# The triangular solve of a gated delta rule: products and subtractions of half the columns

## The chip, the cores and the metric

The kernel runs on one core of a Trainium2 chip. A core has a matrix engine (TensorE, PE in the profile; its weight loads are listed apart, as PEld), a vector engine (VectorE, DVE), an activation engine (ScalarE, ACT), a general engine (GpSimd, POOL), and a sync engine (SyncE, SP) that starts the transfers. Matrix products read their two operands from the on-chip memory SBUF and write to the accumulator memory PSUM, which has 8 banks of 512 fp32 columns on 128 partitions. The metric is the device time of one execution in microseconds; lower is better.

## The reference, cut to what matters

The model is a two-layer trunk that runs over 1024 prompt tokens and 64 tokens of a continued stream. The second layer mixes tokens with a gated delta rule of 8 heads, computed in chunks of 64 tokens:

```python
m = jnp.where(strict, jnp.einsum('bhnid,bhnjd->bhnij', kb, k) * decay, 0.0)
a = m + jnp.eye(L, dtype=f32)
rhs = jnp.concatenate([v * beta[..., None], kb * jnp.exp(G)[..., None]], -1)
sol = lax.linalg.triangular_solve(a, rhs, left_side=True, lower=True, unit_diagonal=True)
w_val, k_cd = sol[..., :dv], sol[..., dv:]
...
def step(st, inp):
    qd, kcd, wv, at, kt, gt = inp
    v_new = wv - jnp.einsum('bhld,bhde->bhle', kcd, st)
    o = jnp.einsum('bhld,bhde->bhle', qd, st) + jnp.einsum('bhij,bhje->bhie', at, v_new)
    st = st * gt[..., None, None] + jnp.einsum('bhld,bhle->bhde', kt, v_new)
    return st, o
```

For each head and chunk a unit lower triangular 64 x 64 matrix `a` has to be inverted. Around this lie the projections, the attention of the first layer and two convolutional feed-forward networks.

## The kernel before

The program is a row of blocks: the first projections, attention, a layer block (`eo`), the delta block (`delta_block`, line 2804), and a second layer block (`oo`). Outside the delta block the work is long rows of matrix products.

**The delta block** takes the chunks in pairs: `Pair(0)` to `Pair(7)` hold two chunks of the prompt each (`nb` = 2, J = 8 matrices on each half of the partitions), `Pair(8)` holds the one chunk of the continued stream (`nb` = 1). Every engine has its own function `run(A, B, C)`, called by `stages` for successive pairs: A is the pair whose matrix is being inverted, B the pair before, whose state update is made, C the pair after, whose inputs are prepared. The order on each engine is the order of the code, and the engines meet at semaphores. Head h of 0 to 3 lies on partitions 0 to 63, head h + 4 on partitions 64 to 127 (`places`), so that two 64 x 64 products run side by side. A chunk is `b`, and `HALVES[b]` are its four matrices per half.

**The inverse** is built by doubling. `T` holds the inverse of the diagonal blocks, `TT` (`solved(A)`) its transpose. Block size 2 is done by masks, then levels l = 1 to 5 double it. At level l, for each chunk b:

- PE, line 3236 ("X product"): `X = ML[l-1]^T T`, 8 products of 64 x 64, to PSUM;
- ACT, line 3339: copies X to SBUF;
- PE, line 3250: the update of T, and line 3253: the update of TT, 8 products each, into the two halves of PSUM bank 6 + b. At level 5 only the second is made;
- DVE, lines 3465 and 3466: subtract them from T and from TT. One semaphore, `Y`, is raised after both groups of a chunk.

PE first issues the X products of both chunks, then the updates of both. It waits for `T` of the chunk before its X products, and for `TT` and the copy `Xs` before its updates. An fp32 product shows as two weight loads and two matmuls in the trace, so a group of 8 products is `x16`.

Between the levels other work is queued on the engines. On DVE `differences(C)` (lines 3376, 3378, 3379) stands after level 1, and `normed(B)` (line 3405) after level 5. On PE `squares_sum(B)` (line 3152) stands after level 2, and the next pair begins with line 3184. On ACT stand `squares_o`, `squares_q`, the decays, `root_o`, `squares_k` and `rms`. POOL makes line 3061 and the masks `ML` (line 2997), scales q (line 3069), and prepares C. In the last pair PE makes some products of the next block (`early`, lines 160 to 166) before and after the X product of level 5.

Of the kernel before, what the change touches and what calls it, by code (L numbers as in the profile page):

```python
# [7 lines left out]
ALU = mybir.AluOpType  # L8
# [64 lines left out]
def settle(eng, sem):  # L73


    eng.sem_inc(sem, 1)
# [2727 lines left out]
def delta_block(nc, ctx, m, d):  # L2804
# [7 lines left out]
    s = m.next  # L2812
    H, L = HEADS, CH
    GR = H // 2
    HALVES = (slice(0, GR), slice(GR, H))
    X_BANK = [None, 0] + [4] * (LEVELS - 2)
    with ExitStack() as mem:
# [17 lines left out]
        TT = (TT, sb("TT1", [P, H, L]))  # L2835
# [6 lines left out]
        def solved(p):  # L2842

            return GB[:, 1] if p.k == NPAIR else TT[p.odd]
# [9 lines left out]
        def bank2(b, n=P):  # L2854

            return m.ps[:, b:b + 2, :].rearrange("p b (h c) -> p (b h) c", c=P)[:, :, 0:n]

        def chunks(x, p):

            return x[:, 0:p.nb].rearrange("p b h g c -> p (b h g c)")  # L2860
# [5 lines left out]
        def bank1(b):  # L2866

            return m.ps[:, b, :].rearrange("p (h c) -> p h c", c=L)
# [223 lines left out]
        def _(pe):  # L3092
            def old_values(B, b):

                pe.wait_ge(s("kc"), B.th(1, 1))
                if not B.first:

                    pe.wait_ge(s("oln"), B.th(0, 1))
                pe.wait_ge(s("S"), B.th(b + 1, 2))
                if B.k == NPAIR:  # L3100
                    pe.wait_ge(s("S_in"), 16)
                r = B.blocks()[b]
                for h, half, j in places(b):
                    ins = pe.matmul(bank2(0)[half, j, :], kc[B.odd][:, h, r], state(B, b)[:, h, :], start=True, stop=True)
                ins.then_inc(s("kS"), 1)

                pe.wait_ge(s("qd"), B.th(1, 1))

                pe.wait_ge(s("onorm"), B.th(1, 1))
                for h in range(H):  # L3110
                    pe.matmul(bank2(2)[:, h, r], state(B, b)[:, h, :], kq[B.odd][:, h, r], start=h % GR == 0, stop=False)

            def solve(B, b):

                pe.wait_ge(s("r"), B.th(b + 1, 2))
                pe.wait_ge(s("TT"), B.th(B.group(LEVELS - 1, b), 2 * LEVELS))
                for h, half, j in places(b):
                    ins = pe.matmul(bank2(0)[half, j, :], solved(B)[half, j, :], vt[B.odd][half, j, :], start=True, stop=True)
                ins.then_inc(s("Tr"), 1)
# [51 lines left out]
            def turn(A, bank, x, name):  # L3171
                settle(pe, s("settled_pe"))
                for b in range(A.nb):
                    for hh in range(GR):
                        ins = pe.transpose(bank2(bank)[:, GR * b + hh, :],
                                           x[:, b, hh].rearrange("p g c -> p (g c)"), m.ident[:, :])
                ins.then_inc(s(name), 1)

            def run(A, B, C):
                if A:  # L3180
                    n = A.n
                    pe.wait_ge(s("sqk"), A.th(1, 1))
                    for b in range(A.nb):
                        ins = pe.matmul(bank2(4)[:, HALVES[b], :], m.ones[:, :], sq[:, HALVES[b], :],
                                        start=True, stop=True)
                    ins.then_inc(s("ksum"), 1)
                    pe.wait_ge(s("in2"), A.loaded())
                    if not A.first:

                        pe.wait_ge(s("TT"), A.th(0, 2 * LEVELS))  # L3190
                    turn(A, 6, kv, "vturned")
                if B:
                    old_values(B, 0)
                    solve(B, 0)
                if not A:
                    early(0, 2)
                if A:
                    pe.wait_ge(s("kn"), A.th(1, 1))
                    pe.wait_ge(s("vt"), A.th(1, 1))
                    gram_k(A)  # L3200
                if B:
                    state_step(B, 0, A)
                    output(B, 0)
                if A:
                    pe.wait_ge(s("in0"), A.th(16, 16))
                    gram_q(A)
                if B and B.n == P:
                    old_values(B, 1)
                    solve(B, 1)
                if A:  # L3210

                    pe.wait_ge(s("T0"), A.th(1, 1))
                    pe.wait_ge(s("AT"), A.th(1, 1))
                    turn(A, 6, kk, "kturned")
                if B and B.n == P:
                    state_step(B, 1, A)
                    output(B, 1)
                if A:

                    if B:  # L3220
                        pe.wait_ge(s("vn"), B.th(B.nb, 2))
                    for l in range(1, LEVELS):
                        pe.wait_ge(s("ML"), A.th(l, LEVELS - 1))
                        if l == 2:

                            if B:
                                pe.wait_ge(s("S"), B.th(3, 2))
                            else:
                                pe.wait_ge(s("kln"), A.th(1, 1))
                        if A.k == NPAIR and l == LEVELS - 1:  # L3230
                            early(0, 0, 1)
                        for b in range(A.nb):
                            pe.wait_ge(s("T"), A.th(A.group(l - 1, b), 2 * (LEVELS - 1)))
                            settle(pe, s("settled_pe"))
                            for h, half, j in places(b):
                                ins = pe.matmul(bank1(X_BANK[l] + b)[half, j, :], ML[half, l - 1, j, :], T[half, j, :],
                                                start=True, stop=True)
                            ins.then_inc(s("X"), 1)
                        if A.k == NPAIR and l == LEVELS - 1:
                            early(0, 1, 2)  # L3240
                        if l == 1:

                            pe.wait_ge(s("kscaled"), A.th(A.nb, 2))
                        for b in range(A.nb):
                            pe.wait_ge(s("TT"), A.th(A.group(l - 1, b), 2 * LEVELS))
                            pe.wait_ge(s("Xs"), A.th(A.group(l - 1, b), 2 * (LEVELS - 1)))
                            settle(pe, s("settled_pe"))
                            if l < LEVELS - 1:
                                for h, half, j in places(b):
                                    pe.matmul(bank1(6 + b)[half, j - GR * b, :], solved(A)[half, j, :], X[half, j, :],  # L3250
                                              start=True, stop=True)
                            for h, half, j in places(b):
                                ins = pe.matmul(bank1(6 + b)[half, GR + j - GR * b, :], X[half, j, :], solved(A)[half, j, :],
                                                start=True, stop=True)
                            ins.then_inc(s("Y"), 1)
                        if B and l == 2:
                            squares_sum(B)
                elif B:
                    early(1)
                    squares_sum(B)  # L3260
                    pe.wait_ge(s("oln"), B.th(1, 1))
                    early(2)
# [107 lines left out]
        def _(dve):  # L3370
# [37 lines left out]
            def run(A, B, C):  # L3408
                if A:
                    n, J, tt = A.n, A.J, solved(A)  # L3410
# [47 lines left out]
                if A:  # L3458
                    for l in range(1, LEVELS):
                        for b in range(A.nb):  # L3460
                            hs = HALVES[b]
                            y = bank1(6 + b)
                            dve.wait_ge(s("Y"), A.th(A.group(l - 1, b), 2 * (LEVELS - 1)))
                            if l < LEVELS - 1:
                                dve.tensor_tensor(T[:, hs], T[:, hs], y[:, 0:GR], ALU.subtract).then_inc(s("T"), 1)
                            dve.tensor_tensor(tt[:, hs], tt[:, hs], y[:, GR:H], ALU.subtract).then_inc(s("TT"), 1)
                        if l == 1 and C:

                            dve.wait_ge(s("kscaled"), A.th(A.nb, 2))
                            dve.wait_ge(s("AT"), A.th(1, 1))  # L3470
                            differences(C)
                        if B and l == rms_level(A):
                            normed(B)
                elif B:
                    normed(B)
# [120 lines left out]
```

## Time and profile before

| | us |
|---|---|
| time, median of 3 runs | 2986.32 (2986.07 to 2988.32) |
| time of the profiled execution | 2987.46 |
| its span | 2985.6 |
| PE busy in the span | 2890.9 (97%) |
| PE weight loads busy | 2765.5 (93%) |
| DVE busy | 1863.9 (62%) |
| POOL busy | 1465.8 (49%) |
| ACT busy | 835.2 (28%) |
| delta block, about | 1786 to 2118 |

Busy time is the sum of the durations of an engine's instructions with overlaps counted once. A weight load overlaps the matmul before it. Times in the rows below are microseconds from the start of the span. The duration of a row of several instructions runs from the start of the first to the end of the last.

### The profile page before, as it was taken

The page shows a single profiled execution, that of the slowest core. Times are in us where ns is not written, and L with a number is a line of the kernel's source. Part 1 is how long each engine was busy: PE and PEld are TensorE (multiplying, and loading weights), DVE is VectorE, ACT ScalarE, POOL GpSimd, SP SyncE. Part 2 cuts the span into 40 slices and gives each one's busy share as a digit, 9 for nine tenths or more (in the row PEclk, how much of TensorE's full clock was granted, in tenths as well). Part 3 has the DMA queues.
Part 4 walks back from the last instruction along what each step waited for, and adds up shares of the span by engine and source line. Part 5 has one row for each costly group of instructions (what it writes and reads, how often), then busy time and mean ns, then how long its engine had stood idle before and what let it go on. Part 6 is the DMA issues. An engine that isn't in the chain of part 4 may idle for free. (4 is left out here: it accounts for less than half of the span.)

```text
span 2985.6 us, 55765 instructions
## 1 busy us (share of the span) xinstructions
PE 2890.9 (97%) x23320; PEld 2765.5 (93%) x23320; DVE 1863.9 (62%) x3041; ACT 835.2 (28%) x1560; POOL 1465.8 (49%) x1026
## 2 busy tenths in 40 slices
PE   8999999999999999999999979999999999999998
PEld 7999767999999999998999978887999999999998
DVE  2337675685555676677887426666487555657666
ACT  2212475233232321112222123433133323231011
POOL 2233101347676752225932227888546777763224
PEclk9999999999999999999999989999999999999999
DMA  6120102022222242212333324332412222224222
GB/s 182 45 59 16 50 2 89 8 81 66 80 74 80 74 163 104 92 45 89 110 94 97 97 73 113 91 90 52 135 41 84 73 80 73 80 88 155 88 81 75
DMA packets 278416, 243.82 MB, mean 82 GB/s; under 512 B 51305, under 2 KB 251351, under 8 KB 277655
## 3 DMA queue, kind: packets, MB, share of 16 engines
q1 hardware_dynamic: 278167, 240.26, 26.2%
q8 instruction: 186, 3.05, 0.4%
q14 instruction: 63, 0.52, 0.1%
HBM read 177.32 MB, written 62.91 MB: 80 GB/s over the span
## 5 line engine op out<-in xcount | busy, mean ns | idle before, releaser
L160 PE MATMUL ps<-xhi,whi 128*128 128x364 f32 x2352 | 781.3, 332 | 9.4 <-PEq L922 3.6
L161 PE MATMUL ps<-xlo,whi 128*128 128x364 f32 x2352 | 774.9, 329 | 0.0
L166 PE MATMUL ps<-xhi,wlo 128*128 128x364 f32 x2352 | 773.9, 329 | 0.0
L160 PEld LDWEIGHTS ps<-xhi,whi 128*128 128x128 f32 x2352 | 441.7, 188 | 15.1 <-issue 8.9
L161 PEld LDWEIGHTS ps<-xlo,whi 128*128 128x128 f32 x2352 | 442.0, 188 | 3.0
L166 PEld LDWEIGHTS ps<-xhi,wlo 128*128 128x128 f32 x2352 | 441.6, 188 | 1.4
L1619 POOL TENSOR_SCALAR whi<-wraw 128x1024 fp32r<-128x1024 f32 x88 | 115.4, 1312 | 571.4 <-PE ps L166 518.6
L1893 PE MATMUL ps<-xhi,wlo 128*128 128x272 f32 (+1 forms) x1216 | 352.4, 290 | 0.0
L1892 PE MATMUL ps<-xlo,whi 128*128 128x272 f32 (+1 forms) x1216 | 352.2, 290 | 0.0
L1891 PE MATMUL ps<-xhi,whi 128*128 128x272 f32 (+1 forms) x1216 | 351.2, 289 | 0.0
L2408 DVE TENSOR_TENSOR z<-ps,z 128x364 f32<-128x364 f32 x384 | 202.9, 535 | 144.6 <-PE ps L166 144.6
L1622 POOL TENSOR_TENSOR wlo<-wraw,whi 128x1024 fp32r<-128x1024 f32 x88 | 234.3, 2662 | 7.3
L1891 PEld LDWEIGHTS ps<-xhi,whi 128*128 128x128 f32 x1216 | 230.2, 189 | 0.0
L1893 PEld LDWEIGHTS ps<-xhi,wlo 128*128 128x128 f32 x1216 | 229.7, 189 | 0.0
L1892 PEld LDWEIGHTS ps<-xlo,whi 128*128 128x128 f32 x1216 | 229.3, 189 | 0.0
L1647 POOL TENSOR_TENSOR wlo<-wraw,whi 128x512 fp32r<-128x512 f32 x114 | 153.0, 1342 | 108.9 <-ACT whi L2186 108.9
L1616 POOL TENSOR_SCALAR z<-z,par 128x364 f32<-128x364 f32 x72 | 62.2, 877 | 138.2 <-DVE xlo L2383 138.1
L2690 DVE SCALAR_TENSOR_TENSOR eo_conv<-eo_raw,par,eo_conv 128x1092 f32<-128x1092 f32 x72 | 123.1, 1709 | 2.6
L1647 POOL TENSOR_TENSOR wlo<-eo_wsum,whi 128x512 fp32r<-128x512 f32 x76 | 98.8, 1310 | 17.8 <-ACT whi L2186 17.8
L1647 POOL TENSOR_TENSOR wlo<-oo_wsum,whi 128x512 fp32r<-128x512 f32 x76 | 99.2, 1316 | 16.8 <-ACT whi L2186 16.8
L2211 ACT CAST xhi<-xlo 128x1092 fp32r<-128x1092 f32 x28 | 30.8, 1105 | 256.0 <-DMA xlo<-hidden 256.0
L421 POOL TENSOR_SCALAR whi<-wraw 128x1024 fp32r<-128x1024 f32 (+2 forms) x22 | 21.7, 989 | 158.1 <-PE ps L166 131.9
(515 smaller groups left out, 6724.6 us busy)
## 6 DMA issues: line engine op xcount, KB each, us to landing
wraw<-in_w_ff_in SPq DMA_DIRECT2D x88, 512.0 KB, 4.6
wraw<-in_w_ff_out SPq DMA_DIRECT2D x44, 512.0 KB, 4.2
qkvz<-eo_ob SPq DMA_DIRECT2D x32, 546.0 KB, 3.0
wraw<-in_w_in_o SPq DMA_DIRECT2D x32, 512.0 KB, 4.4
xlo<-hidden SPq DMA_DIRECT2D x28, 546.0 KB, 5.3
hidden<-eo_ups SPq DMA_DIRECT2D x18, 546.0 KB, 2.8
hidden<-oo_ups SPq DMA_DIRECT2D x18, 546.0 KB, 2.9
z<-residual SPq DMA_DIRECT2D x6, 1456.0 KB, 9.4
```

Of the source, the lines that this page charges most:

```text
L160: one = pe.matmul(out, whi, xhi, start=start, stop=False)
L161: two = pe.matmul(out, whi, xlo, start=False, stop=False)
L166: return pe.matmul(out, wlo, xhi, start=False, stop=stop)
L1616: pool.tensor_scalar(z, z, b, 1.0 if r < SPL else ALPHA, ALU.add, ALU.mult).then_inc(s("z_done"), 1)
L1619: pool.tensor_scalar(hi, x, 1.0, 1.0, ALU.mult, ALU.mult).then_inc(s("w_hi"), 1)
L1622: pool.tensor_tensor(lo, x, hi.bitcast(F32), ALU.subtract).then_inc(s("w_lo"), 1)
L1647: pool.tensor_tensor(lo, source(i, j), hi.bitcast(F32), ALU.subtract).then_inc(s("op_lo"), 1)
L1891: pe.matmul(out, hi[:, c], xh, start=first, stop=False, skip_group_check=True)
L1892: pe.matmul(out, hi[:, c], xl, start=False, stop=False, skip_group_check=True)
L1893: ins = pe.matmul(out, lo[:, c], xh, start=False, stop=k == HQ - 1, skip_group_check=True)
L2408: dve.tensor_tensor(z, m.ps[:, seq % RING, 0:NS], z, ALU.add).then_inc(s("out_free"), 1)
L2690: dve.scalar_tensor_tensor(cv[:, :], x[:, 1 + t:1 + t + TW], one("dconv", t), cv[:, :], ALU.mult, ALU.add).then_inc(s("taps"), 1)
```

## The change

At level l the matrix T consists of blocks of size c = 2^l. The product that is subtracted from T is nonzero only in the columns of even blocks, that from TT only in the columns of odd blocks: 32 of 64 each. The changed kernel computes and subtracts these columns alone. The operand that streams (X or TT) is read with the level's stride, c columns of every 2c. The products of 32 columns are packed side by side: those for T in columns 0 to 127 of the bank, those for TT in columns 256 to 383. DVE subtracts the packed 128 columns from the same 128 columns of T or TT, with the stride. The stationary operand (TT or X) keeps its 64 columns. The X products, their copies, all waits and all other work are as they were.

The number of instructions and their order are the same on every engine. On PE the streaming side of the groups of lines 3250 and 3253 goes from 64 to 32 columns, on DVE each subtraction goes from 128 x 256 to 128 x 128 elements. In the built program DVE's forms are 128x64x2 at level 1, 128x32x4 at level 2, 128x16x8 at level 3, 128x8x16 at level 4 and 128x4x32 at level 5.

```diff
+        def half_columns(x, l, odd):
+
+            return x.rearrange("p (g two c) -> p g two c", two=2, c=1 << l)[:, :, odd, :]
+
+        def half_heads(x, l, odd):
+
+            return x.rearrange("p h (g two c) -> p (h g) two c", two=2, c=1 << l)[:, :, odd, :]
+
+        def packed(b, part):
+
+            return m.ps[:, b, 256 * part:256 * part + GR * L // 2].rearrange("p (h c) -> p h c", c=L // 2)
+
+        def spread(b, part, l):
+
+            return m.ps[:, b, 256 * part:256 * part + GR * L // 2].rearrange("p (h g c) -> p (h g) c", h=GR, c=1 << l)
...
                             if l < LEVELS - 1:
                                 for h, half, j in places(b):
-                                    pe.matmul(bank1(6 + b)[half, j - GR * b, :], solved(A)[half, j, :], X[half, j, :],
-                                              start=True, stop=True)
+                                    pe.matmul(packed(6 + b, 0)[half, j - GR * b, :], solved(A)[half, j, :],
+                                              half_columns(X[half, j, :], l, 0), start=True, stop=True)
                             for h, half, j in places(b):
-                                ins = pe.matmul(bank1(6 + b)[half, GR + j - GR * b, :], X[half, j, :], solved(A)[half, j, :],
-                                                start=True, stop=True)
+                                ins = pe.matmul(packed(6 + b, 1)[half, j - GR * b, :], X[half, j, :],
+                                                half_columns(solved(A)[half, j, :], l, 1), start=True, stop=True)
                             ins.then_inc(s("Y"), 1)
...
-                            y = bank1(6 + b)
                             dve.wait_ge(s("Y"), A.th(A.group(l - 1, b), 2 * (LEVELS - 1)))
                             if l < LEVELS - 1:
-                                dve.tensor_tensor(T[:, hs], T[:, hs], y[:, 0:GR], ALU.subtract).then_inc(s("T"), 1)
-                            dve.tensor_tensor(tt[:, hs], tt[:, hs], y[:, GR:H], ALU.subtract).then_inc(s("TT"), 1)
+                                th = half_heads(T[:, hs], l, 0)
+                                dve.tensor_tensor(th, th, spread(6 + b, 0, l), ALU.subtract).then_inc(s("T"), 1)
+                            th = half_heads(tt[:, hs], l, 1)
+                            dve.tensor_tensor(th, th, spread(6 + b, 1, l), ALU.subtract).then_inc(s("TT"), 1)
```

## Rows read from the trace of the kernel before

**Rows 1.** Windows view (stretch, length, busy PE, PEld, DVE, ACT, POOL), page's slices.
```profile
1786.00:2118.00 332.00, 309.32 (x5974) 269.50 (x5970) 206.52 (x316) 120.91 (x195) 271.94 (x182) 0.98 0.37 91
PE   8999999999999999999999979999999999999998
PEclk9999999999999999999999989999999999999999
```

**Rows 2.** Timeline (start, duration, engine, line), PE's loads, levels 4, 5 of Pair(3).
```profile
1913.90 0.58 PEld L3236 LDWEIGHTS ps<-dn_T,dn_ML 64*64 64x64 f32 x16
1914.73 0.57 PEld L3236 LDWEIGHTS ps<-dn_T,dn_ML 64*64 64x64 f32 x16 [0.25 <-issue]
1915.19 0.58 PEld L3250 LDWEIGHTS ps<-dn_X,dn_TT 64*64 64x64 f32 x16
1915.65 0.58 PEld L3253 LDWEIGHTS ps<-dn_TT,dn_X 64*64 64x64 f32 x16
1916.12 0.58 PEld L3250 LDWEIGHTS ps<-dn_X,dn_TT 64*64 64x64 f32 x16
...
1917.05 0.58 PEld L3236 LDWEIGHTS ps<-dn_T,dn_ML 64*64 64x64 f32 x16
1917.88 0.57 PEld L3236 LDWEIGHTS ps<-dn_T,dn_ML 64*64 64x64 f32 x16 [0.25 <-issue]
...
1919.07 0.57 PEld L3253 LDWEIGHTS ps<-dn_TT,dn_X 64*64 64x64 f32 x16 [0.15 <-issue]
```

**Rows 3.** The timelines of DVE and of ACT in the same stretch.
```profile
1917.34 0.42 DVE L3465 TENSOR_TENSOR dn_T<-dn_T,ps 128x256 f32<-128x256 f32 x1 [0.18 <-PE ps L3253]
1918.63 0.37 ACT L3339 COPY dn_X<-ps 128x256 f32<-128x256 f32 x1 [0.45 <-PE ps L3236]
```

**Rows 4.** Forms and durations (ns, minimum/median/maximum) of loads and matmuls, by line.
```profile
L3250 PEld LDWEIGHTS ps<-dn_X,dn_TT x1024: 128/135/224, 1796.2 to 2063.4; 64*64 64x64 f32 x171
L3134 PEld LDWEIGHTS ps<-dn_AT,dn_vn x256: 188/188/189, 1819.6 to 2082.2; 64*128 64x128 f32 x128
L3134 PE MATMUL ps<-dn_AT,dn_vn x256: 217/272/273, 1819.7 to 2082.2; 64*128 64x64 f32 x128
L3128 PE MATMUL ps<-dn_vn,dn_ktl x272: 271/272/374, 1818.7 to 2105.7; 64*128 64x128 f32 x136
```

**Rows 5.** The timeline of PE's weight loads just ahead of level 1 of Pair(3).
```profile
1900.21 0.97 PEld L3128 LDWEIGHTS ps<-dn_vn,dn_ktl 64*128 64x128 f32 x16 [0.17 <-issue]
1901.10 0.98 PEld L3134 LDWEIGHTS ps<-dn_AT,dn_vn 64*128 64x128 f32 x16
```

**Rows 6.** DVE's groups by form (busy us, mean ns, idle before), 1780 to 2110.
```profile
L3466 DVE TENSOR_TENSOR dn_TT<-dn_TT,ps 128x256 f32<-128x256 f32 x80 | 33.2, 414 | 10.5 <-PE ps L3253 10.5
L3465 DVE TENSOR_TENSOR dn_T<-dn_T,ps 128x256 f32<-128x256 f32 x68 | 28.5, 419 | 56.8 <-PE ps L3253 56.7
L3441 DVE TENSOR_TENSOR dn_TT<-dn_TT,masks 128x512 f32<-128x512 f32 x8 | 13.1, 1642 | 0.0
L3434 DVE TENSOR_TENSOR dn_T<-ps,masks 128x512 f32<-128x512 f32 x8 | 5.5, 682 | 0.0
```

**Rows 7.** The timeline of PE's loads, DVE and ACT in Pair(8), one chunk alone.
```profile
2092.20 0.42 DVE L3465 TENSOR_TENSOR dn_T<-dn_T,ps 128x256 f32<-128x256 f32 x1 [3.44 <-PE ps L3253]
2092.69 0.57 PEld L3236 LDWEIGHTS ps<-dn_T,dn_ML 64*64 64x64 f32 x16 [0.67 <-issue]
2093.44 0.37 ACT L3339 COPY dn_X<-ps 128x256 f32<-128x256 f32 x1 [1.51 <-PE ps L3236]
2093.88 0.57 PEld L3250 LDWEIGHTS ps<-dn_X,dn_gb 64*64 64x64 f32 x16 [0.62 <-issue]
```

**Rows 8.** The timelines of DVE, POOL and PE's loads after level 1 of Pair(3).
```profile
1906.30 1.32 DVE L3376 TENSOR_TENSOR dn_gb<-dn_gb,gcol 128x512 f32<-128x512 f32 x1
1910.37 0.41 DVE L3465 TENSOR_TENSOR dn_T<-dn_T,ps 128x256 f32<-128x256 f32 x1
1904.72 2.36 POOL L3061 TENSOR_TENSOR dn_sq<-dn_sq,dn_qs 128x1024 f32<-128x1024 f32 x1 [3.51 <-ACT dn_sq L3280]
1910.85 1.28 PEld L3236 LDWEIGHTS ps<-dn_T,dn_ML 64*64 64x64 f32 x32 [1.02 <-issue]
1908.67 1.98 PE L3152 MATMUL ps<-dn_sq,ones 128*128 128x512 f32 x4
```

**Rows 9.** The timeline of DVE in Pair(0), where POOL is idle at that place.
```profile
1799.34 0.69 DVE L3376 TENSOR_TENSOR dn_gb<-dn_gb,gcol 128x512 f32<-128x512 f32 x1
```

## The prediction

> **What bounds the kernel now.** I read the engine lines first: PE is busy in every slice of the span at full clock, so time can only be won where PE itself waits or where its own work shrinks. The change touches the delta block alone, 332 us of the span, where PE is busy 309 us and no other engine more than 272 us [rows 1]. Next I read the timeline of PE's weight loads through the levels, since their starts show when PE goes on. Over level 4 of Pair(3) the groups of 16 start 0.46 to 0.47 us apart, but for one hole: the X products of chunk 1 start 0.83 us after those of chunk 0 [rows 2]. One level takes 1917.05 - 1913.90 = 3.15 us: six groups of 0.465 us and this hole of 0.36 us. The hole is a wait for DVE. The subtraction for T of chunk 1 starts at 1917.34, right behind the update products, takes 0.42 us and ends at 1917.76; PE starts chunk 1 at 1917.88 [rows 2, 3].
>
> **The products, PE.** What is halved is the streaming side. Whether a group gets shorter depends on which side sets the pace, and the trace has a pair of lines that tells. Line 3128 has 128 weight columns and 128 streaming ones, line 3134 has 128 and 64. The first takes 1901.10 - 1900.21 = 0.89 us for 16; the 16 loads of the second take 0.98 us, less one load of 0.19 us for 15 steps, about the same spacing (some 55 ns) [rows 5]. Half the streaming columns bought nothing: the matmuls of line 3134 even show the same median of 272 ns [rows 4]. So a pass can't go faster than its weight load. A load of 64 columns takes 135 ns and one of 128 takes 188 ns [rows 4], so loads scale with weight columns, and the 0.465 us per 16 that lines 3250 and 3253 take now is about half of the 0.89 us for weights twice as wide. No row has 64 weight columns beside fewer than 64 streaming ones. The bounds are 0.465 us (nothing saved) and half of it plus the 5 ns by which a step (58 ns for the two halves) exceeds its 53 ns of stream, 0.26 us. I take 0.465 us, because line 3134 is the same case at twice the width. The strided read of X and TT is hidden likewise: 32 columns have the time of 64.
>
> The Trainium skill, page "TensorE: Matmul & The Clock Gate", section "LDWEIGHTS (loading the stationary operand)", says that a load's time follows the columns of the stationary operand, P / 1.2 ns; for 64 columns that is 53 ns. This rule speaks against a gain on PE, and no run here yet shows it for 32 streaming columns; by it the sum is the forecast, while a rule by streaming columns alone gives the first rival.
>
> **The subtractions, DVE.** 512 columns from PSUM take 0.682 us, 256 take 0.419 us [rows 6], so 256 columns cost 0.263 us and 128 cost 0.132 us. A subtraction of 128 columns should take 0.419 - 0.132 = 0.287 us. Strides of 2 to 32 columns have no row. The lower bound is 0.287 us; for the upper I take the dearest rate per column on DVE, 1.642 us for 512 columns in line 3441, 3.2 ns per column [rows 6], with the fixed 0.155 us: 0.155 + 128 x 3.2 ns = 0.565 us. I take 0.287 us: like lines 3465 and 3466 now, the changed ones read one operand from PSUM, while line 3441 reads both from SBUF. So each T is ready 0.132 us earlier.
>
> The Trainium skill, page "Vector Engine (DVE) Microarchitecture Reference", section 5.2, says that a port streams at its full rate if the words come in adjacent pairs from an 8-byte boundary, with any hop between. Level 1, the finest, has just such pairs. By this rule the sum is the forecast; with the row of line 3441 instead it is the slower rival.
>
> **What becomes of 0.132 us per T.** On one chunk alone the chain has no other cover: a T ends at 2092.62 and PE starts at 2092.69, 0.07 us later, and X products to updates take 2093.88 - 2092.69 = 1.19 us (products, copy by ACT to 2093.81, 0.07 us) [rows 7]. This 1.19 us is what comes late next. At level 4 of Pair(3) the X products of chunk 0 start at 1913.90, so the updates can't start before 1915.09; they start at 1915.19 [rows 2]. Though T of chunk 1 comes 0.132 us earlier, PE gains only 0.10 us per level and then waits for ACT's copy.
>
> By level, for a pair of two chunks:
> - Level 3 sets the base, since all before it is swallowed. DVE has `differences` there, and its start doesn't decide: line 3376 takes 1.32 us where POOL is at work and 0.69 us where it isn't [rows 8, 9]. It ends at 1907.62, 0.54 us after POOL's line 3061 at 1907.08. I read this as DVE waiting for POOL's instruction to end, so that starting 0.27 us earlier (two shorter subtractions) changes nothing and T of level 3 starts at 1910.37 as before. T itself is 0.13 us shorter, and PE starts the X products at 1910.72 instead of 1910.85. The squares that PE makes ahead of them (line 3152, from 1908.67 on [rows 8]) move some 0.08 us earlier with level 2 and leave room for that. Gain 0.13 us.
> - Level 4: 0.10 us.
> - Level 5: its last group starts after ACT's copy of chunk 1 (1918.63 + 0.37 + 0.07 = 1919.07) [rows 2, 3], and this copy follows the X products of chunk 1, which wait for T: gain 0.13 us.
>
> Together 0.36 us per pair, 8 pairs: 2.9 us. Pair(0) has no work of POOL there, Pair(7) smaller `differences`; I count them alike. Pair(8) has the open chain: 0.13 us at two level changes, the others lie behind squares or early products, 0.3 us. The next pair starts behind the last group, so the gain is passed on: line 3184 and all behind it wait for PE. POOL at 272 of 332 us has 60 us of slack [rows 1], and covers it. Line 3405 follows the last subtraction and also moves earlier. The sum is 3.2 us. Against the profiled 2987.46 us that is 2984.3 us; that execution is 1.1 us above the median, so for the median **2986.3 - 3.2 = 2983.1 us**.
>
> **Rivals.**
> 1. The stream sets the pace of a group, 0.26 us instead of 0.465 us. For it: 64 and 64 columns are balanced now, and no row is below. Against: line 3134. Level 4 would have four shorter groups, 0.82 us, level 3 likewise, level 5 some 0.3 us, while level 2 is swallowed by `differences`: about 2.1 us per pair, 17 us, **2969 us**.
> 2. Both caps are missing: an earlier start of `differences` is passed on, up to where the squares hold PE (0.2 us more), and ACT's copies come earlier than I read them, so that each T gives its 0.13 us twice over (0.3 us more). 0.36 + 0.5 = 0.9 us per pair, **2979 us**. For it: the holes are 0.36 us wide. Against: the 0.07 us after ACT's copy, seen in the open chain [rows 7].
> 3. Slower: the strided subtraction costs 0.565 us. Each T is then 0.146 us later, at level 3 three in a row: (2 + 1 + 1 + 1 + 1) x 0.146 = 0.9 us per pair, 7 us, **2993 us**. It decides from the point where 128 strided columns take more than 0.42 us, 2.1 ns per column. For it: some DVE rows do cost 3.2 ns per column. Against: those have both operands in SBUF.
> 4. The halved work does what it says, but nothing is left: the copies arrive 0.1 us later than in the open chain and every hole stays. **2986 us**.
>
> **How the numbers follow.** The forecast (gain of 0.5 to 6 us) gets 0.68; rival 1, 0.12; rival 2 (over 6 us), 0.08; rival 3, 0.07; rival 4, 0.05. About 0.2%, 6 us, is what a measurement can tell from no change. Faster is 1 and 2, 0.20; the same is the forecast and 4, 0.73; slower is 3, 0.07. The range runs from 2976.5 us, which takes in rival 2, to 2987.5 us, rival 4 with the runs' own spread; rivals 1 and 3 are left out, 0.19.
>
> **What would show it.** The loads of lines 3250 and 3253 in groups 0.465 us apart as before; the subtractions at about 0.29 us, with the same value at every stride; the hole before chunk 1 at 0.23 us and a new one of about 0.10 us before the first update of chunk 0; `differences` ending at the same distance from line 3061; each pair some 0.36 us shorter. Groups of 0.3 us, or subtractions over 0.42 us, would make the prediction wrong.

## The result

| | before | changed |
|---|---|---|
| time, median of 6 runs | 2986.2 us (2985.45 to 2989.88) | 2996.16 us (2995.06 to 3001.65) |
| ratio to before | 1 | 1.0031 [1.0021, 1.0042] |
| profiled execution / its span | 2987.46 / 2985.6 us | 2995.06 / 2993.2 us |

The changed kernel is 10 us slower, where 3 us of gain were forecast. The two profiled executions are 7.6 us apart: that of the changed kernel is the fastest of its six. Its line numbers are 16 higher than before up to the first subtraction: the X products are line 3252, the updates lines 3266 and 3269, the subtractions 3481 and 3483.

I looked at three places: the levels of Pair(3), where the forecast had its sum, the starts of the pairs, and TensorE's clock.

**The levels do what was forecast.** Timelines of the changed kernel in Pair(3): PE's weight loads from level 3 to level 5, two copies of ACT (of level 3 and of level 5), and then a subtraction, `differences` and POOL's instruction beside it. They answer to [rows 2, 3] and [rows 8].

```profile
1918.56 1.04 PEld L3252 LDWEIGHTS ps<-dn_T,dn_ML 64*64 64x64 f32 x32 [1.02 <-issue]
1919.75 0.57 PEld L3266 LDWEIGHTS ps<-dn_X,dn_TT 64*64 64x64 f32 x16
...
1921.61 1.24 PEld L3252 LDWEIGHTS ps<-dn_T,dn_ML 64*64 64x64 f32 x32
1922.81 0.57 PEld L3266 LDWEIGHTS ps<-dn_X,dn_TT 64*64 64x64 f32 x16
1923.27 0.58 PEld L3269 LDWEIGHTS ps<-dn_TT,dn_X 64*64 64x64 f32 x16
1923.73 0.58 PEld L3266 LDWEIGHTS ps<-dn_X,dn_TT 64*64 64x64 f32 x16
...
1924.67 1.24 PEld L3252 LDWEIGHTS ps<-dn_T,dn_ML 64*64 64x64 f32 x32
1925.86 1.23 PEld L3269 LDWEIGHTS ps<-dn_TT,dn_X 64*64 64x64 f32 x32
```
```profile
1919.31 0.84 ACT L3355 COPY dn_X<-ps 128x256 f32<-128x256 f32 x2 [1.76 <-PE ps L3252]
...
1926.09 0.37 ACT L3355 COPY dn_X<-ps 128x256 f32<-128x256 f32 x1 [0.29 <-PE ps L3252]
```
```profile
1913.44 0.29 DVE L3481 TENSOR_TENSOR dn_T<-dn_T,ps 128x128 f32<-128x128 f32 x1 [0.45 <-PE ps L3269]
1913.84 1.63 DVE L3392 TENSOR_TENSOR dn_gb<-dn_gb,gcol 128x512 f32<-128x512 f32 x1
1912.55 2.37 POOL L3077 TENSOR_TENSOR dn_sq<-dn_sq,dn_qs 128x1024 f32<-128x1024 f32 x1 [3.50 <-ACT dn_sq L3296]
```

With 32 streaming columns the update groups still start 0.46 us apart (1922.81, 1923.27, 1923.73). The subtraction takes 0.29 us. A level takes 1924.67 - 1921.61 = 3.06 us, instead of 3.15 us [rows 2]. Its X products take 1.24 us for 32 loads, against 1.04 us where the same 32 follow without a hole (at 1918.56): the hole ahead of chunk 1 is 0.20 us wide, instead of 0.36 us. At level 3 the updates of chunk 0 now start 0.07 us after ACT's first copy (1919.31 + 0.37 = 1919.68, then 1919.75): this is the wait that the forecast named as next. And `differences` (line 3392) ends at 1915.47, 0.55 us after POOL's instruction at 1914.92, as it ended 0.54 us after it before. The 0.30 us by which it starts earlier, measured from POOL's end, are spent in waiting: it takes 1.63 us instead of 1.32 us.

The subtractions by form, minimum, median and maximum in ns, over all five strides:

```profile
L3481 DVE TENSOR_TENSOR dn_T<-dn_T,ps x68: 272/289/291, 1798.5 to 2103.3; 128x128 f32<-128x128 f32 x68
L3483 DVE TENSOR_TENSOR dn_TT<-dn_TT,ps x80: 273/281/290, 1798.7 to 2073.5; 128x128 f32<-128x128 f32 x80
```

**The pairs do not all do so.** The first X products of level 1 mark each pair. These are PE's loads in the kernel before, then in the changed one: Pair(0), the start of Pair(1), the start of Pair(8), and a product of the next block, the one that stands behind a wait of 1.68 us in both.

```profile
1794.44 1.81 PEld L3236 LDWEIGHTS ps<-dn_T,dn_ML 64*64 64x64 f32 x32 [0.57 <-issue]
1797.46 0.56 PEld L3250 LDWEIGHTS ps<-dn_X,dn_TT 64*64 64x64 f32 x16
1797.93 0.56 PEld L3253 LDWEIGHTS ps<-dn_TT,dn_X 64*64 64x64 f32 x16
...
1829.12 1.01 PEld L3236 LDWEIGHTS ps<-dn_T,dn_ML 64*64 64x64 f32 x32
...
2082.41 0.55 PEld L3236 LDWEIGHTS ps<-dn_T,dn_ML 64*64 64x64 f32 x16
...
2118.25 0.19 PEld L160 LDWEIGHTS ps<-xhi,whi 128*128 128x128 f32 x1 [1.68 <-issue]
```
```profile
1794.71 1.82 PEld L3252 LDWEIGHTS ps<-dn_T,dn_ML 64*64 64x64 f32 x32 [0.43 <-issue]
1797.30 1.00 PEld L3269 LDWEIGHTS ps<-dn_TT,dn_X 64*64 64x64 f32 x16
1798.15 1.00 PEld L3266 LDWEIGHTS ps<-dn_X,dn_TT 64*64 64x64 f32 x16
1799.01 1.00 PEld L3269 LDWEIGHTS ps<-dn_TT,dn_X 64*64 64x64 f32 x16
...
1837.68 0.43 PEld L3252 LDWEIGHTS ps<-dn_T,dn_ML 64*64 64x64 f32 x12
...
2089.29 0.54 PEld L3252 LDWEIGHTS ps<-dn_T,dn_ML 64*64 64x64 f32 x16
...
2126.43 0.19 PEld L160 LDWEIGHTS ps<-xhi,whi 128*128 128x128 f32 x1 [1.69 <-issue]
```

| us | before | changed | difference |
|---|---|---|---|
| start of Pair(0)'s level 1 | 1794.44 | 1794.71 | +0.27 |
| Pair(0) | 34.68 | 42.97 | +8.29 |
| Pairs 1 to 7 together | 253.29 | 251.61 | -1.68 |
| Pair(8) to the next block | 35.84 | 37.14 | +1.30 |
| the rest of the span | | | -0.58 |
| span | 2985.6 | 2993.2 | +7.6 |

In these two executions Pair(0) has nearly the whole loss. Its groups of 16 start 0.86 us apart (1797.30, 1798.15, 1799.01), where those of before start 0.47 us apart.

**The clock.** The granted clock is the share of its full speed at which TensorE was clocked in a stretch. Windows view of Pair(0), before and then changed. The columns are stretch, length, busy time with count of PE, PEld, DVE, ACT and POOL, TensorE's granted clock, DMA share and GB/s; 1.00 is 2.4 GHz and 0.50 is 1.2 GHz.

```profile
1784.00:1797.00 13.00, 8.15 (x119) 7.65 (x121) 6.56 (x9) 1.74 (x4) 13.00 (x11) 0.50 0.48 105
1797.00:1808.00 11.00, 10.45 (x335) 9.99 (x333) 6.31 (x17) 5.20 (x10) 7.29 (x7) 1.00 0.45 120
1808.00:1822.00 14.00, 13.62 (x236) 11.48 (x231) 7.59 (x13) 4.88 (x7) 8.68 (x7) 1.00 0.46 114
```
```profile
1784.00:1791.00 7.00, 3.68 (x64) 3.52 (x64) 2.53 (x3) 2.10 (x3) 7.00 (x7) 0.51 0.41 113
1791.00:1794.00 3.00, 0.55 (x5) 0.58 (x6) 2.86 (x5) 0.00 (x0) 3.00 (x4) 1.00 0.44 93
1794.00:1808.00 14.00, 13.80 (x253) 13.57 (x253) 4.62 (x14) 4.23 (x9) 8.56 (x7) 0.51 0.36 87
1808.00:1815.00 7.00, 5.42 (x167) 5.13 (x165) 1.94 (x8) 1.96 (x4) 6.96 (x6) 0.99 0.66 205
1815.00:1822.00 7.00, 7.00 (x56) 4.76 (x54) 0.58 (x2) 1.38 (x3) 0.84 (x1) 0.52 0.02 5
```

Before, the clock is at the low level for one stretch of these windows, while PE waits a third of the time ahead of the updates, and it is full from 1797 on. Changed, it rises at 1791, falls again at 1794, behind a wait of PE of 3.2 us, and stands at 0.51 for 14 us **in which PE is busy for 13.80 us**, with X products and narrow updates; it drops again for 7 us at 1815, and from 2094.7 to 2098.1 in Pair(8). In the page's slices this is hardly visible: one more digit is 8 than in [rows 1]. Whether the narrow products cause it, or a mere shift of the waits, the trace can't tell.

### The profile page after: what moved, and what is told of

It is laid out like the page before. It is cut to its first block and busy times, and to the rows that moved or that the text cites. A ratio compares the mean times of both kernels' runs of the same rounds, so it can differ in the third digit from the quotient of the medians.

```text
span 2993.2 us, 55765 instructions
## 1 busy us (share of the span) xinstructions
PE 2899.9 (97%) x23320; PEld 2773.7 (93%) x23320; DVE 1862.8 (62%) x3041; ACT 835.9 (28%) x1560; POOL 1467.2 (49%) x1026
```

## The experiments

All ratios are to runs of the kernel before on the same chips. Two switches, by pair, serve nearly all of them: `PE_HALF` packs the products into 32 columns, `DVE_HALF` makes the subtractions read and write half the columns, from the packed products or with a stride from the full ones. `narrow` in the code below is `PE_HALF(A)`. Shown against the changed kernel, the rest of the code being as it was:

```diff
+PE_HALF = lambda p: ...
+DVE_HALF = lambda p: ...
...
+                            y = bank1(6 + b)
+                            if PE_HALF(A):
+                                y0, y1 = spread(6 + b, 0, l), spread(6 + b, 1, l)
+                            elif DVE_HALF(A):
+                                y0, y1 = half_heads(y[:, 0:GR], l, 0), half_heads(y[:, GR:H], l, 1)
+                            else:
+                                y0, y1 = y[:, 0:GR], y[:, GR:H]
```

### Which part of the change costs the time

Theory: the narrow products lower the clock. Rival: the strided or packed access, on PE or DVE. **a1_dve_half** leaves the products at 64 columns in all pairs; **a2_edges_full** does so in Pairs 0 and 8 alone; **a3_contig** streams 32 adjacent columns in place of the strided ones; **a4_pair0_half** is the kernel before with the whole change in Pair(0) only.

```diff
 a1_dve_half
+PE_HALF = lambda p: False
+DVE_HALF = lambda p: True
 a2_edges_full
+PE_HALF = lambda p: p.k not in (0, NPAIR)
+DVE_HALF = lambda p: True
 a3_contig
-                                              half_columns(X[half, j, :], l, 0), start=True, stop=True)
+                                              X[half, j, 0:L // 2], start=True, stop=True)
...
-                                                half_columns(solved(A)[half, j, :], l, 1), start=True, stop=True)
+                                                solved(A)[half, j, L // 2:L], start=True, stop=True)
 a4_pair0_half
+PE_HALF = lambda p: p.k == 0
+DVE_HALF = lambda p: p.k == 0
```

> DVE's half of the change alone: PE computes all 64 columns as in the kernel before, DVE subtracts only the 32 that change, from PSUM with the level's stride. Clock theory (half as many streaming columns keep TensorE at its lower clock in Pair(0) and once in Pair(8)): the clock of the block is as before (low until about 1797 us, not until 1822), Pair(0) takes 34.3 us instead of 43.0, and the time is that before less the gain of the pairs: some 3 us under it, 2983 us. Rival (the strided subtraction or the waits of Pair(0) cost the time): Pair(0) stays at 40 us or more and the time at 2994 us or more.

> The changed kernel, but in Pair(0) and in Pair(8) PE computes all 64 columns; DVE subtracts 32 everywhere. Clock theory: Pairs 1 to 7 don't lose their clock, since the state update of the pair before keeps PE busy; 2983 us, like the run with DVE's half alone. If the half-width products cost something in every pair: 2988 to 2995 us.

> The changed kernel, but the streaming operand of both updates is 32 adjacent columns instead of 32 with the level's stride (so the values computed are others; the work is the same). Clock theory: as the changed kernel, 2996 us, with the low clock until about 1822 us. Rival (the strided read by PE is the cost): back to 2983 us.

> The kernel before, but Pair(0) has the whole change (PE and DVE). Clock theory: nearly all the loss is here, Pair(0) takes 43 us instead of 34.7, the time is 8 us over that before, 2994 us; Pair(8) stays at its full clock. Rival (a loss in every pair): 2987 us.

The kernel before stood at 2987.17 us beside them.

| | median us | ratio |
|---|---|---|
| a1_dve_half | 2983.43 | 0.9989 [0.9980, 0.9997] |
| a2_edges_full | 2985.34 | 0.9993 [0.9984, 1.0001] |
| a3_contig | 3001.88 | 1.0048 [1.0031, 1.0066] |
| a4_pair0_half | 2991.68 | 1.0016 [1.0007, 1.0025] |

Windows of a1_dve_half in Pair(0), then of a4_pair0_half in Pair(0), then of a3_contig in Pair(0), Pair(8) and the first products of the next block:

```profile
1795.00:1799.00 4.00, 3.80 (x76) 3.62 (x76) 1.33 (x3) 0.74 (x2) 4.00 (x4) 0.57 0.66 136
1799.00:1809.00 10.00, 9.85 (x313) 9.38 (x310) 4.71 (x17) 5.20 (x10) 7.02 (x7) 1.00 0.41 108
```
```profile
1793.00:1807.00 14.00, 13.80 (x261) 13.65 (x260) 4.59 (x13) 4.24 (x9) 8.53 (x8) 0.51 0.38 93
```
```profile
1798.00:1838.00 40.00, 36.19 (x797) 32.63 (x795) 22.76 (x43) 14.25 (x24) 25.38 (x19) 1.00 0.42 98
2091.00:2098.00 7.00, 6.50 (x52) 3.92 (x52) 0.49 (x2) 1.00 (x2) 6.64 (x6) 0.51 0.01 2
2101.00:2118.00 17.00, 16.59 (x127) 14.79 (x128) 3.35 (x6) 2.69 (x4) 13.28 (x7) 0.51 0.55 135
```

With full-width products (a1) the clock is back at 1.00 from 1799 on, Pair(0) takes 34.50 us, and the whole kernel is 3.7 us faster, where the forecast had 3.2 us. With the change in Pair(0) alone (a4) the 14 us at 0.51 are there again, Pair(0) takes 39.72 us and the kernel loses 4.5 us; 43 us and 8 us were expected. Adjacent columns (a3) lose at least as much as strided ones, so PE's strided read is not the cause (the values that a3 computes are others). But a3 shows something that I hadn't expected: its Pair(0) ran at full clock, and Pair(8) and the products after it ran at 0.51. Pair(8) can cost more than the changed kernel's profile showed. a2 was expected to stand with a1 and came out 1.9 us above it, with intervals that overlap. One drop stood in the middle of it, in Pair(4), beside narrow products:

```profile
1952.00:1956.00 4.00, 4.00 (x91) 4.00 (x89) 1.06 (x5) 1.42 (x4) 1.98 (x2) 0.57 0.03 6
```

### Filling PE's waits, Pair(8) alone, and one product alone

If it is the engine's own activity that lowers the clock, products of constants placed into PE's waits should raise it again, with the narrow products kept. **c1_after_filled** is the changed kernel with such products, whose results nobody reads, in Pairs 0 and 8; **c2_dve_half_filled** is a1 with the same; **c3_pair8_half** is the kernel before with the change in Pair(8) only; **c4_t_narrow** is a1 with T's products alone at 32 columns.

```diff
 c1_after_filled, c2_dve_half_filled
+            def fill(bank, n, wide):
+
+                if wide:
+                    pe.matmul(m.ps[:, bank, 0:n].rearrange("p (a c) -> p a c", c=P), m.ones[:, :],
+                              m.ones[:, :].unsqueeze(1).to_broadcast([P, n // P, P]), start=True, stop=True)
+                else:
+                    for g in range(2):
+                        r = slice(L * g, L * (g + 1))
+                        pe.matmul(m.ps[r, bank, 0:n].rearrange("p (a c) -> p a c", c=P), m.ones[r, 0:L],
+                                  m.ones[r, :].unsqueeze(1).to_broadcast([L, n // P, P]), start=True, stop=True)
...
                     turn(A, 6, kv, "vturned")
+                    if A.k == 0:
+                        fill(2, 512, True)
+                        fill(3, 512, True)
...
                     gram_q(A)
+                    if A.k == 0:
+                        fill(2, 512, True)
...
+                        if A.k == NPAIR and l < LEVELS - 1:
+                            fill(1 if l == 1 else 5, 256, False)
...
                             ins.then_inc(s("Y"), 1)
+                        if A.k == NPAIR and l < LEVELS - 2 and l != 2:
+                            fill(1 if l == 1 else 5, 256, False)
 c3_pair8_half
+PE_HALF = lambda p: p.k == NPAIR
+DVE_HALF = lambda p: p.k == NPAIR
 c4_t_narrow
-                                    if narrow:
+                                    if True:
                                         pe.matmul(packed(6 + b, 0)[half, j - GR * b, :], solved(A)[half, j, :],
...
-                                y0, y1 = half_heads(y[:, 0:GR], l, 0), half_heads(y[:, GR:H], l, 1)
+                                y0, y1 = spread(6 + b, 0, l), half_heads(y[:, GR:H], l, 1)
```

> The changed kernel with its narrow products, plus products of constants into unused PSUM where PE waits: three of 512 columns ahead of the levels of Pair(0), and pairs of 256 columns after the X products and the updates of Pair(8). Clock theory: it isn't the narrow products in themselves but what PE streams in all, so PE is at its upper clock when the levels of Pair(0) begin and in Pair(8); the time comes back by 8 us or more of the 10, to 2984 to 2988 us. Rival (the narrow form costs in itself): 2996 us or more, since only work was added.

> DVE's half of the change alone (PE computes 64 columns), plus the same filling products. Clock theory: the low clock from 1784 to 1797 us also ends earlier, 1 to 3 us under the version without filling, 2981 to 2983 us. Rival (PE waits for others at that place anyway, and filling delays it): 2984 to 2986 us.

> The kernel before, but Pair(8) alone has the whole change. Clock theory: a low stretch of some us appears behind its level 2 in some of the runs, 1 to 3 us over the kernel before, 2988 to 2990 us. Rival (the chain of one chunk only gets shorter): 2987 us or less.

> As DVE's half alone, and of the two updates on PE only that of T has 32 columns, that of TT has 64. Clock theory: a part of the loss, between 2984 and 2994 us, with a low stretch in Pair(0) that is longer than that of the kernel before. If the streamed columns don't matter: 2983 us.

The kernel before stood at 2987.94 us.

| | median us | ratio |
|---|---|---|
| c1_after_filled | 2989.87 | 1.0004 [0.9995, 1.0013] |
| c2_dve_half_filled | 2986.78 | 0.9992 [0.9983, 1.0001] |
| c3_pair8_half | 2997.91 | 1.0027 [1.0018, 1.0036] |
| c4_t_narrow | 2985.74 | 0.9993 [0.9984, 1.0002] |

Windows of c3_pair8_half, over Pair(8) and the first products of the next block, and its loads at two places there; then the same stretches of the kernel before; then c1_after_filled in Pair(0) and Pair(8):

```profile
2089.00:2096.00 7.00, 6.50 (x52) 3.87 (x52) 0.49 (x2) 1.00 (x2) 6.65 (x6) 0.51 0.01 2
2096.00:2099.00 3.00, 1.88 (x52) 1.61 (x48) 0.49 (x2) 1.52 (x3) 0.00 (x1) 1.00 0.00 0
2099.00:2116.00 17.00, 16.66 (x128) 14.86 (x129) 3.35 (x6) 2.63 (x4) 13.28 (x7) 0.51 0.51 137
```
```profile
2113.54 0.33 PEld L168 LDWEIGHTS ps<-xhi,wlo 128*128 128x128 f32 x1
2113.84 0.33 PEld L162 LDWEIGHTS ps<-xhi,whi 128*128 128x128 f32 x1
...
2119.93 0.19 PEld L168 LDWEIGHTS ps<-xhi,wlo 128*128 128x128 f32 x1
2120.10 0.19 PEld L162 LDWEIGHTS ps<-xhi,whi 128*128 128x128 f32 x1
```
```profile
2086.00:2093.00 7.00, 5.41 (x104) 3.79 (x101) 1.50 (x4) 2.39 (x4) 6.83 (x6) 1.00 0.01 2
2096.00:2113.00 17.00, 16.22 (x161) 14.70 (x156) 4.07 (x5) 3.12 (x5) 15.68 (x9) 1.00 0.63 171
```
```profile
1793.00:1806.00 13.00, 13.00 (x244) 13.00 (x246) 4.37 (x13) 4.06 (x9) 7.78 (x7) 0.50 0.38 93
2081.00:2107.00 26.00, 25.41 (x383) 20.21 (x380) 7.26 (x14) 7.05 (x11) 21.97 (x14) 1.00 0.27 72
```

For c3 I had expected 1 to 3 us and measured 10 us. The clock is low for 24 us there, and not only beside narrow products: the last narrow group starts at 2104.7, and behind it, up to 2116, PE does full-sized products, those of the next block among them, which start 0.30 us apart at the low level and 0.17 us at the full one. So a drop that begins beside the narrow products is paid for by what stands behind them too. c1 gave back most of the loss, by its median 8 us of 10, though it stayed above the 2984 to 2988 us that were expected. In its trace the clock of Pair(8) was 1.00 throughout, while in Pair(0), against the expectation, 13 us at 0.50 remained, with PE busy in every one of them. That execution is the fastest of eleven, which reach up to 2995.70 us; what the slower ones lost isn't traced. c2 brought nothing beyond a1: the further 1 to 3 us that were expected did not come. c4 lies in its expected range, but the longer low stretch in Pair(0) that was to go with it isn't there: its clock is low from 1784 to 1798, as before. It stands 2.2 us below the kernel before, where a1 stood 3.7 us below, with intervals that overlap. Four of the nine groups of updates are narrow in it, but it is 1.5 us slower than a1 against its kernel before, where the changed kernel is 13 us slower: the loss isn't proportional to the narrow work.

### Products or subtractions, and whether the filling is the cure

**d1_pair8_filled** is c3 with the filling products of Pair(8). **d2_pair8_pe_only** is c3 with the subtractions at full size, as before. **d3_dve_half_again** repeats a1.

```diff
 d1_pair8_filled
+                        if A.k == NPAIR and l < LEVELS - 1:
+                            fill(1 if l == 1 else 5, 256, False)
...
+                        if A.k == NPAIR and l < LEVELS - 2 and l != 2:
+                            fill(1 if l == 1 else 5, 256, False)
 d2_pair8_pe_only
+PE_HALF = lambda p: p.k == NPAIR
+DVE_HALF = lambda p: False
...
-                            if PE_HALF(A):
+                            if False:
                                 y0, y1 = spread(6 + b, 0, l), spread(6 + b, 1, l)
 d3_dve_half_again
+PE_HALF = lambda p: False
+DVE_HALF = lambda p: True
```

> The kernel before with the whole change in Pair(8), as in c3, plus products of constants of 256 columns where PE waits in Pair(8). Clock theory: PE streams enough again, so the low stretches from 2089 us on are gone and with them all of the loss of c3: 2986 to 2989 us instead of 2998. Rival (the narrow products or their packing cost in themselves): 2998 us or more.

> The kernel before, but in Pair(8) PE computes only 32 columns per product, packed, while DVE subtracts 256 columns as before (of which half are stale, so the values are others than the reference's). Clock theory: PE's half alone brings the loss of c3, 2996 to 2999 us. Rival (the loss needs DVE's shorter subtraction as well, or comes from it): 2988 us.

> The version with DVE's half alone a second time, on another visit to a chip, beside the same kernel before. Its gain is that of the shorter subtractions in the waits of PE, some 3 us (ratio 0.999). If the first gain was chance: no difference.

The kernel before stood at 2988.0 us.

| | median us | ratio |
|---|---|---|
| d1_pair8_filled | 2987.48 | 0.9998 [0.9989, 1.0007] |
| d2_pair8_pe_only | 2999.17 | 1.0034 [1.0021, 1.0046] |
| d3_dve_half_again | 2984.99 | 0.9990 [0.9981, 0.9999] |

Windows of d1_pair8_filled in Pair(8), with one of its filling products, and of d2_pair8_pe_only at the two places where c3 was low:

```profile
2084.00:2110.00 26.00, 25.40 (x378) 20.21 (x376) 7.18 (x14) 7.04 (x11) 22.24 (x14) 1.00 0.27 72
```
```profile
2086.94 0.66 PE L3174 MATMUL ps<-ones 64*64 64x256 f32 x4
```
```profile
2089.00:2096.00 7.00, 6.49 (x55) 3.78 (x53) 0.75 (x2) 1.00 (x2) 6.67 (x6) 0.54 0.01 2
2099.00:2116.00 17.00, 16.49 (x134) 14.55 (x130) 3.75 (x6) 2.76 (x4) 13.29 (x7) 0.52 0.47 126
```

d2 loses as much as c3 with the subtractions as before (half of what they subtract is stale there), so it is the products. d1 has the very products of c3, adds work to the bounding engine, and loses nothing: it is PE's activity, not the packed access. The eleven executions of d1 (2984.43 to 2990.02 us) all lie under the eleven of c3 (2990.73 to 2999.66 us). d3 confirms a1: some 3 us under the kernel before, and so some 13 us under the changed one.

### The clock in all thirteen traces

Windows of 1 us give the stretches in which the granted clock was low, here from 1780 us on. The names are shortened; "half" is c4, with T's products alone narrow.

| Pair(0) | low, us | Pair(0) takes |
|---|---|---|
| full width: before, c3, d1, d2 | one stretch, 1783-1797 to 1785-1800 | 34.7 to 35.7 us |
| half: c4 | 1784-1798 | 34.2 us |
| full width: a1, a2, c2, d3 | two, the second 4 to 5 us long (1791-1796 to 1795-1799) | 34.2 to 35.7 us |
| narrow: changed, a4, c1 | two, the second 14 to 15 us long (1792-1807 to 1794-1808); the changed kernel's a third, 1814-1822 | 38.3 to 43.0 us |
| narrow: a3 | one, 1784-1798 | 35.4 us |

| Pair(8) | low, us |
|---|---|
| full width: before, a1, a2, a4, c2, d3; half: c4 | none |
| narrow: changed | 2094-2099 |
| narrow: a3, c3, d2 | 7 to 8 us from 2089 or 2091 on, then 18 us from 2099 or 2101 on |
| narrow and filled: c1, d1 | none |

So in Pair(0) narrow products cost time where the clock fell just ahead of the levels: it then came back some 10 us later than beside full-width ones. Where it had been low without a break since 1783 to 1785, it was full again from 1797 to 1800 on for both, and a3 lost nothing there. In Pair(8) all four traces with narrow products alone have a drop, and none of the nine others. Between the two pairs there are two drops of 4 us, in a3 (1838-1842) and in a2 (Pair(4)), both with narrow products at that place.

The mean granted clock is on record for every execution, not the traced ones alone: 0.985 to 0.987 in the six of the changed kernel, 0.989 to 0.993 in the 82 of the kernel before beside the experiments, 0.990 to 0.992 in the 22 of a1 and d3. The 0.005 between the changed kernel (mean 0.986) and the kernel before (0.991) are 15 us of full speed over 2990 us, by my estimate, against the 13 us between it and a1. At one clock, 0.991, the kernel before takes 2987.6, 2988.2 and 2987.7 us in the mean of the three sets, a1 2983.8 us and d3 2985.3 us: their gain is not one of the clock.

## Why the prediction was wrong

**The mechanism, right.** Groups of 0.46 us against 0.465 us; subtractions of 0.281 to 0.289 us against 0.287 us, at all strides; level 4 shorter by 0.09 us (0.10); `differences` held to 0.55 us behind POOL (0.54). The X products of level 3 start 8.58 us after those of level 1 instead of 8.71 us, a gain of 0.13 us (0.13). At level 5 the last group starts at 1926.53, 0.07 us after ACT's copy of chunk 1 (1926.09 + 0.37) and 1.86 us after the X products, instead of 2.02 us [rows 2], a gain of 0.16 us (0.13). Rivals 1 and 3 fall with these rows, and rival 4 with the hole of 0.20 us. On the hold, the Trainium skill, page "SBUF — State Buffer", section "🔬 SBUF: two separate sides", says that a VectorE operation with two SBUF inputs and a GpSimd operation that reads SBUF block each other for a whole instruction; the 1.63 us of line 3392, which starts 0.30 us earlier against POOL's instruction and ends no earlier, agree.

**The gain per pair, smaller in the sum and unevenly spread.** Pair(3) got shorter by 0.55 us (36.30 to 35.75 us), not by 0.36 us. Its levels give 0.38 us. The rest lies behind them, 0.13 us of it in the wait ahead of line 3160, which shrank from 0.63 to 0.50 us and which the forecast left out. From Pair(1) to Pair(7) the gains are 0.54, 0.18, 0.55, -0.23, 0.59, 0.31 and -0.26 us, 1.68 us in all where the forecast had 7 x 0.36 = 2.5 us. The other traces agree. Between the medians of the five traces with the old subtractions there (before, a4, c3, d1, d2) and of the eight with halved ones the gains are 0.50, 0.19, 0.54, -0.48, 0.60, 0.32 and -0.04 us, 1.63 us in all. In Pair(4) PE stops inside a group, where the program has no wait: at level 5, behind the first 7 loads of chunk 0, the next load starts 1.04 us after the group did in the changed kernel and 0.46 us in the kernel before. It stops at the same loads in both, for different times; why isn't known. So pairs 1 to 7 give 1.6 us where 2.5 us were forecast, Pair(8) 0.25 us of 0.3 us. The gains that a1 and d3 show as a whole, 3.7 and 3.0 us, fit the forecast's 3.2 us, but with intervals of more than 2 us to each side; by the traces some 2.4 us are accounted for, 0.5 us of them in Pair(0), which is less than its spread from trace to trace.

**The step that failed** is the first one: "PE is busy in every slice of the span at full clock", and behind it "half the streaming columns bought nothing", costed at zero. The mean of 0.98 over the block [rows 1] was not full clock, nor is the digit 8 in its slices: 2% of 332 us is 13 us at half the clock, and the windows above show them, 1784 to 1797, just ahead of the first updates. I took the clock for something that the change couldn't touch. A group bound by its weight load has the same time with half the stream, but it streams half the columns, and in the two pairs where PE has its widest waits (Pair(0) has no pair ahead of it, Pair(8) one chunk) the clock fell or stayed low. In place of nothing the runs showed 13 us, the distance from a1 to the changed kernel. At the low clock a group is that slow whatever its width: the narrow ones start 0.86 us apart, and 32 loads of the X products, which kept 64 columns, take 1.71 us (from 1799.86 on), 0.86 us per 16. No rival said this; the one that ended slower, rival 3, put the loss on DVE, whose time was as forecast.

By single pairs the loss adds up: 4.5 us for Pair(0) alone (a4) and 10 us for Pair(8) alone (c3; 8 us by its ratio), less the gain of 3 us, make 11.5 us (or 9.5 us); 10.0 us were measured. The intervals of the parts reach 3 us to each side, so this is as close as they allow.

**What stays open.** Why an execution loses in one pair and not in the other: the profiled one of the changed kernel lost 8.3 us in Pair(0) and 1.3 us in Pair(8), that of a3 had the reverse. In Pair(0) it goes with whether the clock had come back for some us ahead of the levels, and the runs don't show what decides that. The clock's fall is shown to hang on what PE does, by a1, d1 and d2; what exactly about it decides is not.

## What to carry to other kernels

On TensorE, work that costs no time may still hold the clock: before narrowing products in a stretch with waits, read the granted clock by windows of a few us, not as a mean or from the page's slices, and look for a low stretch beside the place that is edited. Halve the work that the bounding engine waits for (here the subtractions on DVE) and leave the products at full width where the weight load sets their pace anyway; that alone was the better kernel, by 3 us of 2987. Where products must be narrow, products of constants in PE's waits can win the clock back, as in Pair(8), but did not do so everywhere.

## What the runs showed of the hardware

- TensorE at 1.2 GHz while busy: 13.80 of 14.00 us in the changed kernel and 13.00 of 13.00 us in c1, with 64x64 fp32 weight loads beside 32 streaming columns. The Trainium skill, page "TensorE: Matmul & The Clock Gate", section "HAM oscillation — how this bites in real kernels", ties falls of the clock to gaps in which TensorE waits. The fall at 1794 came right behind a gap of 3.2 us, which agrees; the one at 1815 came behind 5.42 busy us of 7.00, with no gap over 1.6 us. The rule alone doesn't tell why the clock came back within 4 us beside full-width products (a1) and after 14 us beside narrow ones, and there the runs decide.
- A low clock that begins in Pair(8) lasts on: in c3, full-sized products behind the last narrow group ran at 0.51 for 11 us, those of the next block in steps of 0.30 us instead of 0.17 us.
- With 64 weight columns, 32 streaming columns take the time of 64 (0.46 us per 16 at full clock), and subtractions of 128 columns with strides of 2 to 32 columns all lie within 0.272 to 0.291 us.
